# State space layer of a diffusion trunk: the tile of dt ahead of z's tiles, and out-projection weights ahead of modulation pieces in the load queue

## The chip, the cores and the metric

The kernel runs on one core of a Trainium2 chip. The metric is device time in microseconds (us), the median of several runs. Engines: PE is TensorE (matmul), DVE is VectorE, ACT is ScalarE, POOL is GpSimd, SP issues nearly all DMAs. Every engine runs its own list of instructions in order, and the lists meet only at semaphores.

## The reference, cut to what matters

Four layers, each a token mixer (pooling, state space, conformer, attention) and a convolutional feed-forward part. Two streams of tokens, 128 context and 256 latent, share the weights. The state space mixer (layer 1) and the gated residual around it:

```python
def ssd_mixer(h, h0, w_in, conv_w, conv_b, dt_bias, a_log, d_skip, norm_g, w_out):
    proj = h @ w_in                                   # 1024 -> z 2048, xbc 4096, dt 64
    z = proj[..., :SSD_D_INNER]
    xbc = jax.nn.silu(depthwise_conv(proj[..., SSD_D_INNER:SSD_D_INNER + SSD_CONV_DIM], conv_w, conv_b))
    dt = jax.nn.softplus(dt_raw + dt_bias.astype(jnp.float32))
    a = -jnp.exp(a_log.astype(jnp.float32))
    y_f, s_f = ssd_scan(x, dt[:, :, 0], a[0], bm, cm, h0[:, 0])      # and y_b, s_b backward
    y = (y_f + flip(y_b) + x * skip).reshape(bsz, seq_len, SSD_D_INNER).astype(h.dtype)
    y = rms_norm(y * jax.nn.silu(z), norm_g)
    return y @ w_out, jnp.stack([s_f, s_b], axis=1)
...
def gated_residual(x, out, mod, k, g):
    return x + mod[:, None, 3 * k + 2] * rms_norm(out, g)
```

The scan needs dt, and the cumulative sums of dt * a over each chunk of 128 tokens. It does not need z: z only multiplies the result of the scan. The conformer (layer 2) ends in a product with `conf_w_out` (1024 x 1024). The modulation `mod = silu(cond) @ w_mod[i] + b_mod[i]` is six vectors of 1024 for each layer and stream.

## The kernel before

**Products.** Every weight is fp32 and is split into a rounded high part and a low rest, and every product is three matmuls (high x high, low x high, high x low). The weights come in chunks of 128 x 1024 (512 KB; dt's is half as wide), numbered through the whole kernel by `plan()`. A ring of four slots (`raw`, `w_hi`, `w_lo`) holds them. SP loads chunk m into `raw` once both low halves of chunk m - 4 are made. ScalarE rounds it (`round_to`, L820) once chunk m - 4 has been used by TensorE. GpSimd (`low_to`, L675) and VectorE (L1179) make half of the low part each; for the conformer's weights GpSimd makes all of it. TensorE waits for both (`chunk_ready`). Each engine's calls of `round_to` and `low_to` stand at written-out places between its other work, so a wait for a chunk holds whatever stands behind it on that engine.

**State space layer.** `in_tile` makes 32 tiles for the convolution, then 16 tiles of z (24 matmuls of 386 columns each), then one of dt with 64 rows. ScalarE evacuates z with Silu into `zt` (L937), and dt with a copy (L940). `dt_prepare` is a chain through four engines: three transposes (L1767), VectorE adds the bias and forms -|v| (L1347 to L1350), ScalarE takes Exp (L945), VectorE makes the logarithm by a series (L1352 to L1363, 15 steps), TensorE makes the cumulative sums and totals (L1774, L1775), VectorE subtracts (L1369 to L1373), ScalarE takes two Exp (L947, L948), VectorE multiplies (L1375). Then 24 steps of the scan follow. Afterwards, in `ssd_end`, VectorE multiplies tile m with z (L1463) and forms its low part (L1458), ScalarE squares it (L986) and rounds it (L987), GpSimd adds up the squares (L745), and each engine makes its part of one more weight chunk per tile.

**Out-projections.** `out_product` lets a chunk of weights be the moving operand against three units of 128 tokens (two banks each). All chunks but the last four (`TAIL`) go through all units in turn, 18 matmuls of 512 columns a chunk (L1709 to L1711). The last four are done for unit 0 first, so that its residual and norm can begin (`transition`) while TensorE does units 1 and 2. In the state space layer the sum of squares over partitions (L1867) precedes chunk 12. `fill` puts the products of modulation pieces between the transposes of the transition.

**Modulation pieces.** w_mod comes in pieces of 1 MB (`load_mod`, L511), 12 for the end of one sublayer and the next. They lie in SBUF places that other buffers leave free only at certain times: slots 0 and 1 in the scan's buffers, others under `zt`, `xbc` or the conformer's tables. SP's list interleaves them with chunks of weights by hand. For the out-projection of the state space layer it is:

```python
load_to(s.n0 + 13)
sp.wait_ge(w_used, s.n0 + 6)
load_ends(2, 2, 7)
load_to(s.n0 + 15)
sp.wait_ge(y_lo_ready, KI)
load_ends(2, 4, 5, 6)
load_to(s.n0 + s.chunks)
```

For the conformer's it is four chunks, the wait `sp.wait_ge(mid_lo, KD)`, and then a chunk and two pieces in turn.

Of the kernel before, what the change touches and what calls it, by code (L numbers as in the profile page):

```python
# [11 lines left out]
ACT = mybir.ActivationFunctionType  # L12
AX = mybir.AxisListType

P = 128
D = 1024
KD = D // P
# [75 lines left out]
def plan():  # L93
    order = [Linear("pool", 2)]
    for l in range(DEPTH):
        if l == 1:
            order += [Linear("ssd_conv", CONV_TILES), Linear("ssd_z", KI), Linear("ssd_dt", 1, KD * NDT),
                      Linear("ssd_out", KI)]
        if l == 2:
            order += [Linear("conf_in", 2 * KD), Linear("conf_out", KD)]  # L100
        if l == 3:
            order += [Linear("qk", QK), Linear("v", 2), Linear("attn_out", KD)]
        order += [Linear(f"ffn_in{l}", FFN_TILES), Linear(f"ffn_out{l}", KF)]
# [34 lines left out]
def build_trunk(nc, a, out):  # L138
# [4 lines left out]
    with ExitStack() as ctx:  # L143
# [146 lines left out]
        def tile_bank(j):  # L290
            return bank((j + 2) % 4)
# [129 lines left out]
        EVAC_Z, EVAC_DT = 0, KI  # L421
# [31 lines left out]
        ALL_STEPS = list(steps())  # L453

# [48 lines left out]
        def _(sp):  # L503
# [85 lines left out]
            for n, s in enumerate(order[1:], 1):  # L589
# [23 lines left out]
                elif s.name == "ssd_out":  # L613
# [7 lines left out]
                    load_to(s.n0 + 15)  # L621
                    sp.wait_ge(y_lo_ready, KI)
                    load_ends(2, 4, 5, 6)
                    load_to(s.n0 + s.chunks)
# [42 lines left out]
        def _(pool):  # L667
# [142 lines left out]
        def _(act):  # L810
# [122 lines left out]
            def ssd_z_dt():  # L933
                s = lin["ssd_z"]
                for m in range(KI):
                    act.wait_ge(w_used, s.n0 + m + 1)
                    act.activation(zt[:, m, :], tile_bank(m)[:, 0:COLS], ACT.Silu).then_inc(evac, 1)  # L937
                    round_to(s.n0 + m + 5)
                act.wait_ge(w_used, lin["ssd_dt"].n0 + 1)
                act.activation(dt_columns, tile_bank(KI)[0:NDT, 0:COLS], ACT.Copy).then_inc(evac, 1)  # L940
# [39 lines left out]
            def ssd_end():  # L980
                n0 = lin["ssd_out"].n0
                for m in range(KI):
# [6 lines left out]
                    if m + 3 < KI:  # L989
                        round_to(n0 + m + 3)  # L990
# [139 lines left out]
            for l in range(DEPTH):  # L1130
                if l == 1:
                    ssd_conv()
                    ssd_z_dt()
                    dt_prepare()
                    scan_act()
                    round_to(lin["ssd_out"].n0 + 3)
                    ssd_end()
                    round_to(lin["ssd_out"].n0 + KI)
# [28 lines left out]
        def _(vec):  # L1167
# [154 lines left out]
            def ssd_conv():  # L1322
# [11 lines left out]
                low_to(lin["ssd_dt"].n0 + 1)  # L1334

            def dt_prepare():
# [28 lines left out]
                assert n[0] == DT_DVE - 2  # L1365
                vec.wait_ge(dt_pe, 2)
                cum = bank(7)[:, 0:192].rearrange("p (c h) -> p c h", c=3)
                total = bank(7)[:, 192:384].rearrange("p (c h) -> p c h", c=3)
# [4 lines left out]
                link(vec.tensor_tensor(to_end, full_decay, neg_cum[:, :, :], ALU.add))  # L1373
                vec.wait_ge(dt_act, 4)
# [76 lines left out]
            def ssd_end():  # L1451
# [10 lines left out]
                for m in range(KI):  # L1462
# [3 lines left out]
                    if m + 3 < KI:  # L1466
                        low_to(n0 + m + 3)
# [136 lines left out]
            for l in range(DEPTH):  # L1604
                if l == 1:
# [3 lines left out]
                    low_to(lin["ssd_out"].n0 + 3)  # L1609
                    ssd_end()  # L1610
                    low_to(lin["ssd_out"].n0 + KI)
# [20 lines left out]
        def _(ten):  # L1632
# [130 lines left out]

            def dt_prepare():
                ten.wait_ge(evac, EVAC_DT + 1)
# [3 lines left out]
                ins.then_inc(dt_pe, 1)  # L1769
                ten.wait_ge(z_dt, DT_DVE - 2)  # L1770
                cum = bank(7)[:, 0:192].rearrange("p (c h) -> p c h", c=3)
# [3 lines left out]
                ten.matmul(bank(7)[:, 192:384], ones[:, :], adt[:, :, :].rearrange("p c h -> p (c h)"),  # L1775
                           start=True, stop=True, skip_group_check=True).then_inc(dt_pe, 1)

# [63 lines left out]
            def ssd():  # L1841
                conv, z, dt = lin["ssd_conv"], lin["ssd_z"], lin["ssd_dt"]
# [5 lines left out]
                for m in range(KI):  # L1848
                    if m < 4:
                        ten.wait_ge(conv_done, conv.conv0 + CONV_TILES - 3 + m)  # L1850
                    else:
                        ten.wait_ge(evac, EVAC_Z + m - 3)
                    chunk_ready(z.n0 + m)
                    tile(tile_bank(m)[:, 0:COLS], z.n0 + m, P, slice(0, COLS)).then_inc(w_used, 1)
                chunk_ready(dt.n0)
                ten.wait_ge(evac, EVAC_Z + KI - 3)
                tile(tile_bank(KI)[0:NDT, 0:COLS], dt.n0, NDT, slice(0, COLS)).then_inc(w_used, 1)
# [337 lines left out]
```

## Time and profile before

| What | Value |
|---|---|
| Median of 3 runs | 2193.52 us (2193.38 to 2196.08) |
| Profiled execution, its own time | 2196.92 us |
| Its span, in which all rows below lie | 2195.2 us |
| PE busy | 2015.6 us, 92% |
| DVE, ACT, POOL busy | 58%, 45%, 34% |
| Read from HBM | 314.96 MB, 145 GB/s over the span |

Times in rows are microseconds from the start of the span. A busy share is an average over stages with different limits; what a change in one stage is worth is read from that stage. The state space layer's z tiles lie at 565 to 637, its scan at 651 to 798, its out-projection and transition at 798 to 917; the conformer's out-projection begins at 1364.64.

### The profile page before, as it was taken

Reading aid. Unit: us, or ns where it says so; the run is one execution under the profiler, and the core shown is the slowest. Engines: PE = TensorE matmul, PEld = TensorE weight load, DVE = VectorE, ACT = ScalarE, POOL = GpSimd, SP = SyncE. Lnnn points to the kernel's source line nnn. Section 1 sums busy time; section 2 is a strip of 40 time slices with the busy share of each in tenths; the row PEclk is TensorE's granted clock in tenths of the full one; section 3 lists DMA queues with packets and bytes.
Section 4 is the critical chain, followed back from the end, with each engine's and each line's share of the span. In section 5 each row is a group of like instructions: output and inputs, shape, how many; then the busy total and the mean of one; then the engine's idle time right before and its main releaser. Section 6 shows DMA issues by size and latency. Waiting matters only on the chain.

```text
span 2195.2 us, 30850 instructions
## 1 busy us (share of the span) xinstructions
PE 2015.6 (92%) x11973; PEld 1813.9 (83%) x11973; DVE 1279.9 (58%) x1911; ACT 994.9 (45%) x1767; POOL 747.3 (34%) x568
## 2 busy tenths in 40 slices
PE   3789999999978878899999998799999979899998
PEld 1579998799977866799987997599998766699986
DVE  0567761566328866677724795377751686577732
ACT  1344442554336633544424686354442535544432
POOL 0133324333327655333343840233334320333242
PEclk6889999999989989999999999899999988999999
DMA  9953336433310134643365500643446322243332
GB/s 370 374 212 125 125 120 244 162 121 124 125 62 26 40 120 157 237 144 122 119 225 178 196 19 1 278 173 125 125 163 220 145 109 81 86 144 125 124 126 77
DMA packets 77073, 320.98 MB, mean 146 GB/s; under 512 B 8672, under 2 KB 14208, under 8 KB 63104
## 3 DMA queue, kind: packets, MB, share of 16 engines
q1 hardware_dynamic: 76048, 318.18, 41.3%
q8 instruction: 96, 1.57, 0.3%
q10 hardware_dynamic: 880, 0.82, 0.1%
q14 instruction: 49, 0.40, 0.1%
HBM read 314.96 MB, written 4.01 MB: 145 GB/s over the span
## 4 chain that ended last, share of the span: by engine, by line
PE 77%; DVE 9%; ACT 5%; DMA 4%; issue 2%; POOL 1%; SPq 1%; DVEq 0%; ACTq 0%
PE pair L1675 16%; PE pair L1677 16%; PE pair L1676 16%; PE pair L1709 6%; PE pair L1710 6%; PE pair L1711 6%; DMA mod_more<-in_w_mod 2%; PE pair L1798 2%; DVE x L1246 2%; PE pair L1896 1%; PE pair L1895 1%; PE pair L1894 1%; PE pair L1831 1%; ACT junk L848 1%; DMA raw<-in_ssd_out 1%
## 5 line engine op out<-in xcount | busy, mean ns | idle before, releaser
L675 POOL TENSOR_TENSOR w_lo<-raw,w_hi 128x512 fp32r<-128x512 f32 (+1 forms) x375 | 578.2, 1544 | 1205.5 <-ACT w_hi L820 1205.5
L1675 PE MATMUL pair<-h_hi,w_hi 128*128 128x386 f32 (+1 forms) x2008 | 687.6, 342 | 19.1 <-POOL h_lo L682 19.1
L1677 PE MATMUL pair<-h_hi,w_lo 128*128 128x386 f32 (+1 forms) x2008 | 683.4, 340 | 0.0
L1676 PE MATMUL pair<-h_lo,w_hi 128*128 128x386 f32 (+1 forms) x2008 | 682.8, 340 | 0.0
L1179 DVE TENSOR_TENSOR w_lo<-raw,w_hi 128x512 fp32r<-128x512 f32 x351 | 426.6, 1217 | 335.9 <-ACT w_hi L820 335.9
L820 ACT ACTIVATE w_hi<-raw 128x1024 fp32r<-128x1024 f32 x375 | 393.0, 1050 | 294.2 <-PE pair L1711 213.0
L1675 PEld LDWEIGHTS pair<-h_hi,w_hi 128*128 128x128 f32 (+1 forms) x2008 | 380.6, 190 | 23.6 <-POOL h_lo L682 22.3
L1676 PEld LDWEIGHTS pair<-h_lo,w_hi 128*128 128x128 f32 (+1 forms) x2008 | 381.5, 190 | 0.9
L1677 PEld LDWEIGHTS pair<-h_hi,w_lo 128*128 128x128 f32 (+1 forms) x2008 | 380.8, 190 | 0.3
L1303 DVE SCALAR_TENSOR_TENSOR acc<-pair,taps,acc 128x385 f32<-128x385 f32 x176 | 108.9, 619 | 213.1 <-ACT acc L907 213.1
L907 ACT ACTIVATE acc<-pair,taps 128x386 f32<-128x386 f32 x176 | 117.3, 667 | 236.7 <-PE pair L1677 236.7
L1710 PE MATMUL pair<-w_hi,g 128*128 128x512 f32 x528 | 208.5, 395 | 0.0
L1711 PE MATMUL pair<-w_lo,g 128*128 128x512 f32 x528 | 208.4, 395 | 0.0
L1709 PE MATMUL pair<-w_hi,g 128*128 128x512 f32 x528 | 208.3, 395 | 0.0
L1709 PEld LDWEIGHTS pair<-w_hi,g 128*128 128x128 f32 x528 | 99.2, 188 | 23.4
L1710 PEld LDWEIGHTS pair<-w_hi,g 128*128 128x128 f32 x528 | 99.2, 188 | 23.3
L1711 PEld LDWEIGHTS pair<-w_lo,g 128*128 128x128 f32 x528 | 99.2, 188 | 23.4
L905 ACT ACTIVATE g<-gate 128x386 fp32r<-128x386 f32 x84 | 44.3, 528 | 162.4 <-DVE gate L1316 162.4
L1310 DVE SCALAR_TENSOR_TENSOR acc<-pair,taps,acc 128x385 f32<-128x385 f32 x176 | 108.5, 617 | 3.2
L1484 DVE SCALAR_TENSOR_TENSOR convolved<-glu,conf_tab,convolved 128x400 f32<-128x400 f32 x120 | 101.3, 917 | 0.0
L682 POOL TENSOR_TENSOR h_lo<-stage,h_hi 128x512 fp32r<-128x512 f32 x21 | 31.9, 1521 | 92.7 <-ACT h_hi L870 92.7
L1798 PE MATMUL pair<-mod_raw,wk 128*64 128x128 f32 x384 | 44.8, 291 | 17.9 <-DVE stage L1414 11.3
(254 smaller groups left out, 2557.1 us busy)
## 6 DMA issues: line engine op xcount, KB each, us to landing
raw<-in_ffn_in SPq DMA_DIRECT2D x176, 512.0 KB, 3.5
raw<-in_ffn_out SPq DMA_DIRECT2D x88, 512.0 KB, 3.6
mod_raw<-in_w_mod SPq DMA_DIRECT2D x32, 1024.0 KB, 7.7
mod_base<-in_w_mod SPq DMA_DIRECT2D x31, 1024.0 KB, 7.3
mod_more<-in_w_mod SPq DMA_DIRECT2D x20, 1024.0 KB, 13.8
raw<-in_ssd_conv SPq DMA_DIRECT2D x32, 512.0 KB, 3.5
gb<-rows_dram SPq DMA_DIRECT2D x8, 1024.0 KB, 5.4
raw<-in_ssd_z SPq DMA_DIRECT2D x16, 512.0 KB, 3.5
```

The source lines that it names most:

```text
L675: pool.tensor_tensor(w_lo[:, m % SLOTS, 0:w], raw[:, m % SLOTS, 0:w], w_hi[:, m % SLOTS, 0:w].bitcast(F32), ALU.subtract).then_inc(w_low_p ...
L820: act.activation(w_hi[:, m % SLOTS, 0:w], raw[:, m % SLOTS, 0:w], ACT.Copy).then_inc(w_rounded, 1)
L907: act.activation(acc[:, j % 4, :], tile_bank(j)[:, 0:COLS], ACT.Identity, scale=taps[:, l, j, 1:2], bias=taps[:, l, j, 3:4]).then_inc(acc_ ...
L1179: vec.tensor_tensor(w_lo[:, m % SLOTS, w0:w1], raw[:, m % SLOTS, w0:w1], w_hi[:, m % SLOTS, w0:w1].bitcast(F32), ALU.subtract).then_inc(w_ ...
L1303: vec.scalar_tensor_tensor(out=acc[:, j % 4, 1:COLS], in0=b[:, 0:COLS - 1], scalar=taps[:, l, j, 0:1], in1=acc[:, j % 4, 1:COLS], op0=ALU. ...
L1310: vec.scalar_tensor_tensor(out=acc[:, j % 4, 0:COLS - 1], in0=b[:, 1:COLS], scalar=taps[:, l, j, 2:3], in1=acc[:, j % 4, 0:COLS - 1], op0= ...
L1675: ten.matmul(to, wh, h_hi[:, k, cols], start=k == 0, stop=False, skip_group_check=True)
L1676: ten.matmul(to, wh, h_lo[:, k, cols], start=False, stop=False, skip_group_check=True)
L1677: ins = ten.matmul(to, wl, h_hi[:, k, cols], start=False, stop=k == KD - 1, skip_group_check=True)
L1709: ten.matmul(to, hi[:, k, cols], wh, start=first, stop=False)
L1710: ten.matmul(to, lo[:, k, cols], wh, start=False, stop=False)
L1711: ins = ten.matmul(to, hi[:, k, cols], wl, start=False, stop=last)
```

## The change

- The order of the chunks is conv, dt, z, out in place of conv, z, dt, out.
- TensorE: dt's tile goes to bank 7 right after the convolution's tiles, then z tile 0, the three transposes, z tiles 1 to 3, the cumulative sums (now in bank 5), z tiles 4 to 15. z's tiles rotate over three banks (2, 3, 7) in place of four. Before the scan TensorE waits for the last evacuation of z.
- ScalarE: dt's copy and z's Silus stand inside `dt_prepare`: Exp of a_log, copy of dt, z 0, Exp of -|v|, z 1 to 15, then the last two Exp.
- VectorE: `low_to` calls up to z chunk 5 stand after the 18 steps, and those up to the fourth out-projection chunk before the last step. ScalarE and GpSimd also handle the first four out-projection chunks before the scan (three before, of which GpSimd and VectorE made the low parts after it).
- `ssd_end`: each tile m goes with chunk `min(m + 3, KI)`, so the last chunk is made inside the loop on all three engines.
- SP, `ssd_out`: all 16 chunks are issued ahead of the wait for `y_lo_ready`; the pieces 4, 5, 6 follow it.
- SP, `conf_out`: all 8 chunks are issued ahead of the wait for `mid_lo`; the seven pieces follow it together.

```diff
-            order += [Linear("ssd_conv", CONV_TILES), Linear("ssd_z", KI), Linear("ssd_dt", 1, KD * NDT),
+            order += [Linear("ssd_conv", CONV_TILES), Linear("ssd_dt", 1, KD * NDT), Linear("ssd_z", KI),
...
-        EVAC_Z, EVAC_DT = 0, KI
+        EVAC_DT, EVAC_Z = 0, 1
...
+        def z_bank(m):
+            return bank((2, 3, 7)[m % 3])
...
-                    load_to(s.n0 + 15)
+                    load_to(s.n0 + s.chunks)
                     sp.wait_ge(y_lo_ready, KI)
                     load_ends(2, 4, 5, 6)
-                    load_to(s.n0 + s.chunks)
...
-                    load_to(s.n0 + SLOTS)
+                    load_to(s.n0 + s.chunks)
                     sp.wait_ge(mid_lo, KD)
-                    for i in range(KD - SLOTS):
-                        load_to(s.n0 + SLOTS + i + 1)
-                        load_ends(4, 2 + 2 * i, 3 + 2 * i) if i < 3 else load_ends(4, 8)
+                    load_ends(4, *range(2, MOD_SLOTS))
...
-                    if m + 3 < KI:
-                        low_to(n0 + m + 3)
+                    low_to(n0 + min(m + 3, KI))
...
-                    low_to(lin["ssd_dt"].n0 + 1)
+                    low_to(lin["ssd_out"].n0 + SLOTS)
                     pool.wait_ge(z_dt, DT_DVE)
                     scan_pool()
-                    low_to(lin["ssd_out"].n0 + 3)
                     ssd_end()
-                    low_to(lin["ssd_out"].n0 + KI)
...
+            def z_evac(m):
                 s = lin["ssd_z"]
...
+                act.wait_ge(w_used, s.n0 + m + 1)
+                act.activation(zt[:, m, :], z_bank(m)[:, 0:COLS], ACT.Silu).then_inc(evac, 1)
+                round_to(s.n0 + m + 5)
 
             def dt_prepare():
                 act.activation(rowc[:, 960:1024], dt_rows[:, 1, :], ACT.Exp).then_inc(dt_act, 1)
+                act.wait_ge(w_used, lin["ssd_dt"].n0 + 1)
+                act.activation(dt_columns, bank(7)[0:NDT, 0:COLS], ACT.Copy).then_inc(evac, 1)
+                round_to(lin["ssd_dt"].n0 + 5)
+                z_evac(0)
                 act.wait_ge(z_dt, 3)
                 act.activation(rowc[:, 576:768], rowc[:, 384:576], ACT.Exp, scale=-1.0).then_inc(dt_act, 1)
+                for m in range(1, KI):
+                    z_evac(m)
                 act.wait_ge(z_dt, DT_DVE - 1)
...
-                low_to(lin["ssd_dt"].n0 + 1)
+                low_to(lin["ssd_z"].n0 + 4)
...
+                low_to(lin["ssd_z"].n0 + 6)
                 vec.wait_ge(dt_pe, 2)
...
                 link(vec.tensor_tensor(to_end, full_decay, neg_cum[:, :, :], ALU.add))
+                low_to(lin["ssd_out"].n0 + SLOTS)
                 vec.wait_ge(dt_act, 4)
...
+            def z_tiles(first, last):
+                z = lin["ssd_z"]
+                for m in range(first, last):
+                    if m < 2:
+                        ten.wait_ge(conv_done, lin["ssd_conv"].conv0 + CONV_TILES - 3 + m)
+                    else:
+                        ten.wait_ge(evac, EVAC_Z + m - 2 if m > 2 else EVAC_DT + 1)
+                    chunk_ready(z.n0 + m)
+                    tile(z_bank(m)[:, 0:COLS], z.n0 + m, P, slice(0, COLS)).then_inc(w_used, 1)
+
             def dt_prepare():
+                dt = lin["ssd_dt"]
+                chunk_ready(dt.n0)
+                tile(bank(7)[0:NDT, 0:COLS], dt.n0, NDT, slice(0, COLS)).then_inc(w_used, 1)
+                z_tiles(0, 1)
                 ten.wait_ge(evac, EVAC_DT + 1)
...
                 ins.then_inc(dt_pe, 1)
+                z_tiles(1, 4)
                 ten.wait_ge(z_dt, DT_DVE - 2)
...
                            start=True, stop=True, skip_group_check=True).then_inc(dt_pe, 1)
+                z_tiles(4, KI)
+                ten.wait_ge(evac, EVAC_Z + KI)
```

## Rows read from the trace of the kernel before

**Rows 1.** The page's chain that ended last, by engine

```profile
PE 77%; DVE 9%; ACT 5%; DMA 4%; issue 2%; POOL 1%; SPq 1%; DVEq 0%; ACTq 0%
```

**Rows 2.** Windows: length, busy PE, PEld, DVE, ACT, POOL (count), PEclk, DMA share, GB/s

```profile
564.87:637.15 72.28, 72.25 (x408) 70.94 (x407) 11.53 (x16) 25.17 (x36) 23.87 (x14) 1.00 0.35 113
637.15:650.69 13.54, 2.25 (x9) 1.64 (x10) 8.66 (x24) 3.00 (x6) 0.00 (x0) 0.68 0.00 0
868.17:884.48 16.31, 10.85 (x31) 8.57 (x32) 0.87 (x2) 1.32 (x3) 1.76 (x1) 0.71 1.00 404
869.45:873.86 4.41, 4.41 (x12) 3.44 (x12) 0.18 (x1) 0.26 (x1) 0.00 (x0) 0.50 1.02 427
1371.14:1383.60 12.46, 12.46 (x54) 9.97 (x53) 1.05 (x4) 2.48 (x4) 2.75 (x2) 1.00 0.83 329
1385.00:1400.97 15.97, 7.71 (x20) 5.26 (x20) 0.00 (x1) 2.11 (x2) 5.31 (x3) 0.64 1.01 420
```

**Rows 3.** Timeline of all engines, last z tile to scan: start, us, instruction, idle before

```profile
637.15 0.49 ACT L940 ACTIVATE stage<-pair 64x386 f32<-64x386 f32 x1 [2.77 <-PE pair L1677]
637.66 1.28 ACT L943 ACT_TABLE_LOAD   x1
...
638.13 0.36 DVE L1347 TENSOR_TENSOR rowc<-pair,dt_rows 128x192 f32<-128x192 f32 x1 [16.48 <-PE pair L1767]
...
639.67 0.26 DVE L1352 TENSOR_SCALAR rowc<-rowc 128x192 f32<-128x192 f32 x1 [0.50 <-ACT rowc L945]
...
645.87 0.36 DVE L1363 SCALAR_TENSOR_TENSOR adt<-rowc,dtv 128x192 f32<-128x192 f32 x1
...
646.29 1.17 PE L1774 MATMUL pair<-adt,tri 128*128 128x96 f32 x4 [8.20 <-DVE adt L1363]
...
648.25 0.36 DVE L1369 TENSOR_SCALAR neg_cum<-pair 128x192 f32<-128x192 f32 x1 [2.02 <-PE pair L1775]
...
649.47 0.36 ACT L947 ACTIVATE stage<-stage 128x192 f32<-128x192 f32 x1 [9.90 <-DVE stage L1373]
...
650.69 0.45 PE L1819 MATMUL pair<-ident,xbc 128*128 128x128 f32 x1 [2.55 <-DVE stage L1375]
```

**Rows 4.** Timeline of ScalarE, one of 16 z tiles

```profile
573.39 0.49 ACT L937 ACTIVATE zt<-pair 128x386 f32<-128x386 f32 x1 [2.81 <-PE pair L1677]
573.78 1.05 ACT L820 ACTIVATE w_hi<-raw 128x1024 fp32r<-128x1024 f32 x1
```

**Rows 5.** Timeline, out-projection of the state space layer

```profile
844.34 1.04 ACT L820 ACTIVATE w_hi<-raw 128x1024 fp32r<-128x1024 f32 x1
...
846.02 1.66 DVE L1463 TENSOR_TENSOR xbc<-xbc,zt 128x386 f32<-128x386 f32 x1
...
862.52 0.60 ACT L987 ACTIVATE y_hi<-xbc,ssd_cols 128x386 fp32r<-128x386 f32 x1
...
863.27 1.22 DVE L1463 TENSOR_TENSOR xbc<-xbc,zt 128x386 f32<-128x386 f32 x1
...
884.48 1.11 ACT L837 ACTIVATE junk<-pair,ssd_inv 128x1024 bf16<-128x1024 f32 x1 [4.92 <-PE pair L1711]
...
891.55 1.04 ACT L820 ACTIVATE w_hi<-raw 128x1024 fp32r<-128x1024 f32 x1
```

**Rows 6.** Chain that ended last, in order of time, both out-projections: start, us, what

```profile
800.26 10.27 DMA raw<-in_ssd_out
...
868.70 9.78 DMA raw<-in_ssd_out
...
1376.58 17.87 DMA raw<-in_conf_out
...
1400.97 1.24 DVE wk L1233
```

**Rows 7.** Timeline of SP and of GpSimd, conformer's out-projection

```profile
1252.58 119.96 SPq L520 DMA_DIRECT2D raw<-in_conf_out  x5
...
1395.61 2.34 POOL L675 TENSOR_TENSOR w_lo<-raw,w_hi 128x1024 fp32r<-128x1024 f32 x1 [3.83 <-ACT w_hi L820]
```

More of the change, by code:

```diff
@@ L931, in ssd_conv @@
                 act.activation(xbc[:, CONV_TILES - 1, :], xbc[:, CONV_TILES - 1, :], ACT.Silu).then_inc(xbc_ready, 1)
-            def ssd_z_dt():
+            def z_evac(m):
                 s = lin["ssd_z"]
[L935 to L940, printed above, removed]
+                act.wait_ge(w_used, s.n0 + m + 1)
+                act.activation(zt[:, m, :], z_bank(m)[:, 0:COLS], ACT.Silu).then_inc(evac, 1)
+                round_to(s.n0 + m + 5)
             def dt_prepare():
                 act.activation(rowc[:, 960:1024], dt_rows[:, 1, :], ACT.Exp).then_inc(dt_act, 1)
+                act.wait_ge(w_used, lin["ssd_dt"].n0 + 1)
+                act.activation(dt_columns, bank(7)[0:NDT, 0:COLS], ACT.Copy).then_inc(evac, 1)
+                round_to(lin["ssd_dt"].n0 + 5)
+                z_evac(0)
                 act.wait_ge(z_dt, 3)
                 act.activation(rowc[:, 576:768], rowc[:, 384:576], ACT.Exp, scale=-1.0).then_inc(dt_act, 1)
+                for m in range(1, KI):
+                    z_evac(m)
                 act.wait_ge(z_dt, DT_DVE - 1)
@@ L988, in ssd_end @@
                                    ).then_inc(y_hi_ready, 1)
-                    if m + 3 < KI:
-                        round_to(n0 + m + 3)
+                    round_to(n0 + min(m + 3, KI))
                 act.wait_ge(y_sum, 1)
@@ L1132, in _ @@
                     ssd_conv()
-                    ssd_z_dt()
                     dt_prepare()
                     scan_act()
-                    round_to(lin["ssd_out"].n0 + 3)
                     ssd_end()
-                    round_to(lin["ssd_out"].n0 + KI)
                     transition(2, lin["ffn_in1"].n0)
@@ L1365, in dt_prepare @@
                 assert n[0] == DT_DVE - 2
+                low_to(lin["ssd_z"].n0 + 6)
                 vec.wait_ge(dt_pe, 2)
-                cum = bank(7)[:, 0:192].rearrange("p (c h) -> p c h", c=3)
-                total = bank(7)[:, 192:384].rearrange("p (c h) -> p c h", c=3)
+                cum = bank(5)[:, 0:192].rearrange("p (c h) -> p c h", c=3)
+                total = bank(5)[:, 192:384].rearrange("p (c h) -> p c h", c=3)
                 ch.did(vec.tensor_scalar(neg_cum[:, :, :], cum, -1.0, None, ALU.mult))
@@ L1465, in ssd_end @@
                         y_low(m - 1)
-                    if m + 3 < KI:
-                        low_to(n0 + m + 3)
+                    low_to(n0 + min(m + 3, KI))
                 y_low(KI - 1)
@@ L1608, in _ @@
                     scan_dve()
-                    low_to(lin["ssd_out"].n0 + 3)
                     ssd_end()
-                    low_to(lin["ssd_out"].n0 + KI)
                     transition(2, lin["ffn_in1"].n0)
@@ L1769, in dt_prepare @@
                 ins.then_inc(dt_pe, 1)
+                z_tiles(1, 4)
                 ten.wait_ge(z_dt, DT_DVE - 2)
-                cum = bank(7)[:, 0:192].rearrange("p (c h) -> p c h", c=3)
+                cum = bank(5)[:, 0:192].rearrange("p (c h) -> p c h", c=3)
                 for d in range(2):
@@ L1774, in dt_prepare @@
                     ten.matmul(cum[:, :, hs], tri[:, d, :], adt[:, :, hs], start=True, stop=True, skip_group_check=True)
-                ten.matmul(bank(7)[:, 192:384], ones[:, :], adt[:, :, :].rearrange("p c h -> p (c h)"),
+                ten.matmul(bank(5)[:, 192:384], ones[:, :], adt[:, :, :].rearrange("p c h -> p (c h)"),
                            start=True, stop=True, skip_group_check=True).then_inc(dt_pe, 1)
+                z_tiles(4, KI)
+                ten.wait_ge(evac, EVAC_Z + KI)
             def scan_pe():
@@ L1841, in ssd @@
             def ssd():
-                conv, z, dt = lin["ssd_conv"], lin["ssd_z"], lin["ssd_dt"]
+                conv = lin["ssd_conv"]
                 in_start(1)
@@ L1847, in ssd @@
                     in_tile(conv, j, 1)
[L1848 to L1857, printed above, removed]
                 dt_prepare()
```

## The prediction

> **What bounds the kernel now.** I read the chain of work that ended last first [rows 1]: TensorE carries most of it, so a gain has to come from places where TensorE stands still. The busy time by windows [rows 2] shows three such places that the diff touches. Between the last column tile of the state space layer and its scan, 13.54 us hold 2.25 us of matmuls. In its out-projection 16.31 us hold 10.85 us with the DMA engines full. In the conformer's out-projection 15.97 us hold 7.71 us, again with the DMA full. A row of the timeline or the chain then names what ended each wait. All three are serial chains: softplus on ScalarE and VectorE [rows 3], and twice a weight that sits in the queue behind modulation pieces [rows 6].
>
> **Softplus (dt first).** Today TensorE's last product matmul is evacuated at 637.15 and the scan starts at 650.69 [rows 3]: 13.5 us.
>
> What moves: dt's tile costs TensorE the same wherever it stands (17 tiles fill 72.28 us, 4.25 each [rows 2]). Its evacuation, the transposes, 18 VectorE steps and one Exp go under z's tiles. What must hold is that they are done by the time TensorE has z tile 3 behind it. With TensorE's conv tiles ending at 564.87: dt ends at 569.1, z tile 0 at 573.4, the transposes at about 574. Three VectorE steps and the Exp took from 638.13 to 639.67, 1.5 us [rows 3]; up to two table loads of 1.28 come on top. The chain from L1352 to L1363 runs from 639.67 to about 646.25, so 6.6 us [rows 3]. It ends near 583 to 585; z tiles 1 to 3 end at 574.2 + 3 x 4.25 = 586.9. Slack 2 to 4 us, so no stall.
>
> Queued behind it: VectorE's low halves of z chunks 4 and 5, done near 586; they are wanted at 588 and 592. SP's loads of z chunks 8 and 9 wait for them; chunk 8 is first rounded after tile 4 (about 592). ScalarE's rounding waits for the three VectorE steps once, and is otherwise four chunks ahead; a z tile costs it 1.44 us of 4.25 [rows 4], so three banks in place of four and two more table loads fit. I cost these at nothing; were the cover gone, each late us would be paid once.
>
> What stays visible. (a) Between z tiles TensorE now does the transposes and the cumulative sums. The sums took 646.29 to 648.25, 1.96 us, at half clock (the window's granted clock is 0.68 of full [rows 2, 3]). At full clock half of that, 1.0, plus 0.5 for the transposes: 1.5 us, bounds 1.0 and 2.5. (b) After z tile 15: its Silu 0.5, the rounding of an out-projection chunk 0.95 [rows 4], a table load 1.28 since Exp follows Silu, and then the steps that today run from 649.47 to 650.69, 1.22 us [rows 3]. Sum 4.0 us, with 3.7 and 6 as bounds (the VectorE low half of that chunk stands in the same queue before the last product).
> Gain 13.5 - 1.5 - 4.0 = **8.0 us** (5.0 to 8.8).
> The change loads tables five times here, where today it is once (Exp, Silu, Exp, Silu, Exp), and one load stands in the open; the row gives a load 1.28 us, from 637.66 to 638.94 [rows 3]. The Trainium skill (ScalarE: Activation LUTs, Rules for kernel authors) speaks against that: do all functions of one table set before switching, and budget about 2.7 us for a switch. By that figure, an estimate from that page, the open tail would be 1.4 us longer and the whole gain 22.9.
>
> **Out-projection of the state space layer.** VectorE's three low halves at its start leave the end of the scan for z's time. It gains nothing: the next weight, chunk 4, comes behind the gate row and two modulation pieces, 10.27 us after its issue at 800.26 [rows 6]. VectorE's queue blocks on it (its low half stands before the product of tile 3), and SP's order there is untouched. So TensorE merely waits longer, and chunks 2 to 11 keep their times.
>
> The last chunk is another matter. Its load is issued after y_lo's last tile and three pieces, lands 9.78 us later at 878.48, and lets the first output unit start its square at 884.48 [rows 5, 6]. Now it is issued when low half 11 is done (about 847, within 3 us of the rounding at 844.34), so it is there when its slot comes free. The price: its rounding and low halves move in front of y's tiles 14 and 15. ScalarE is free for it at 862.52 + 0.5 = 863.05, when chunk 11 has just been used. From a rounding over the low half to the next VectorE product it takes 846.02 - 844.34 = 1.68 us, so tile 14's product moves from 863.27 to 864.73 [rows 5]. With GpSimd on the same buffers, the two products take about 1 us more: 2.4 us, bounds 1.5 and 3.5. The sums' matmul, with which the window at 868.17 begins, goes to 870.6; 1.3 us later the 24 matmuls of unit 0 begin, the first ten at half clock: the ten that start in the window took 4.41 us (it counts two of the sums' too), and warm 54 took 12.46, so 0.233 each with the edges [rows 2]. 870.6 + 1.3 + 4.4 + 14 x 0.233 + 0.2 for the last one's end = 879.8. Gain 884.48 - 879.8 = **4.7 us** (3 to 6).
> Next late: the first ffn_in weight, behind five pieces whose issue moves with y_lo, 2 to 3 us later than today. 5.8 MB at the 404 GB/s of that window [rows 2] plus some 2 us from 870.5 is 887; ScalarE wants it 891.55 - 884.48 = 7.1 us after unit 0's square [rows 5], near 887. Even, at most 1 us lost.
>
> **Out-projection of the conformer.** Chunks 4 to 7 are each issued in turn with two pieces between them; the last is issued at 1376.58 and lands 17.87 us later [rows 6]. SP issued the first chunks from 1252 on, and the fifth only after the wait on mid_lo, 120 us later [rows 7]. Without that order the slots are free from the low half of chunk 3 on, some 90 us before they are wanted. What paces it then is TensorE itself: the first phase ends at 1383.6 [rows 2]. Chunk 7 is rounded from 1383.8, 1.05; its low half takes GpSimd 2.34 [rows 7]; ready at 1387.3. Unit 0's chunks 4 to 6 are 18 x 0.233 = 4.2 and reach 1387.8, so no wait; six more end at 1389.4. VectorE starts on unit 0 at 1389.4 in place of 1400.97 [rows 6]. From there VectorE and ScalarE pace the transition, so the whole of it moves: **11.6 us** (bounds 9, if half the low halves come late, and 12).
> Next late: the seven pieces, 7.3 MB at 420 GB/s [rows 2], from 1374.3 to 1391.8; today they end later. The first is used after units 1 and 2, 48 matmuls or 11 us after 1389.4 at the soonest, so they cost nothing. The first ffn_in chunk follows by 1393; by the other transition's 7.1 us it is wanted at 1396.5 or later.
>
> **Sum.** 8.0 + 4.7 + 11.6 = 24.3 us. The profiled execution took 2196.92 us for a span of 2195.2, so about 2172.6 after. It lies 3.4 above the median of the runs, against which the forecast stands: 2193.52 - 24.3 = **2169.2 us**, -1.1%.
>
> **Rivals.**
> 1. All three gains, as above: 0.60. Its own range 2166 to 2173.
> 2. The softplus chain surfaces (ScalarE's waits and four table loads hold z's roundings, or the tail has another step): the layer's first gain falls to 3. For it: the slack is only 2 to 4 us, and the chain's two-input steps share time with GpSimd's low halves. Against: one delay is paid once, not per tile. 2193.52 - 19.3 = 2174. Chance 0.15.
> 3. Earlier weights, but the pieces become the wait: both transitions use their pieces soon after. In the conformer the margin is 10 us and in the state space layer about 0 for the first ffn_in weight. Were half of the 16.3 us there given back: 2177.5. Chance 0.10.
> 4. More than forecast: TensorE stands still for only 4 us before the scan, and 8 us of half clock at several restarts go away. The ten slow matmuls of a restart cost 10 x 0.2 = 2 us each, two or three places: 2164. Chance 0.10.
> 5. Slower: VectorE's low halves of z chunks 4 and 5 now stand behind the softplus chain, and TensorE, then every later z tile, waits for them. It decides once the chain ends more than 24 us past 586.9, near 611; the chain would have to take 33 us where 6.6 are measured. At 10 us beyond that point the time is 2203. Chance 0.03.
> 6. None shows, because other stages take it back (a wait that ends at the same time for another reason): 2193. For it speaks that two of the three gains lie in one layer; against, that the chain there names one releaser at a time. Chance 0.02.
>
> **How the numbers follow.** Cases 1 to 4 reach from 2164 to 2177.5 and hold 0.95; leaving out the outer ends of 3 and 4 about 0.85 remains in 2164.5 to 2177. Faster by over 0.2%: 0.95. Within 0.2% (4.4 us, about what a measurement of this kernel can tell from no change): 0.02. Slower: 0.03.
>
> **What would show it.** Scan's first transposes near 642.5 to 644 in place of 650.69, with a table load on ScalarE just before; z tiles without gaps but for one of 1 to 2 us after tile 3; the last ssd_out load issued near 840 to 848 less the shift, and no TensorE wait on a GpSimd low half of 5 us before unit 0; four conf_out loads before 1300 and no wait for them after the first phase. It would be wrong if a z tile waited on a low half, if the tail after z tile 15 exceeded 6 us, or if the first ffn_in weight landed late.

## The result and the profile after

The changed kernel takes 2167.8 us, median of four runs from 2167.5 to 2168.1, beside 2193.5 (2190.3 to 2196.1) for the kernel before in the same measurement: ratio 0.9884, 95% interval 0.9867 to 0.9901, or 25.6 us. The forecast was 2169.2, 24.3 us. Measured again it was 2166.6 beside 2194.3: 0.9873 (0.9858 to 0.9888).

The chain that ended last, by engine, in the page of the changed kernel; it answers to [rows 1]:

```profile
PE 80%; DVE 6%; ACT 4%; issue 3%; DMA 3%; POOL 3%; SPq 1%; DVEq 0%; ACTq 0%; POOLq 0%
```

TensorE's share rose from 77 to 80%. VectorE's fell from 9 to 6%, the DMA's from 4 to 3, and GpSimd's rose from 1 to 3. The windows of the changed kernel (columns as in [rows 2]) show where:

```profile
562.77:636.33 73.56, 73.52 (x417) 71.99 (x415) 25.00 (x41) 31.34 (x42) 28.19 (x17) 1.00 0.36 115
636.33:640.23 3.90, 0.00 (x0) 0.03 (x1) 1.16 (x3) 3.33 (x5) 1.77 (x1) 0.95 0.00 0
858.37:868.02 9.65, 9.65 (x32) 7.94 (x33) 0.45 (x2) 0.98 (x2) 0.00 (x0) 0.65 0.85 336
1369.43:1373.86 4.43, 4.43 (x20) 3.58 (x20) 0.00 (x0) 0.00 (x0) 2.41 (x1) 1.00 0.99 418
```

z's stretch has VectorE 13.5 us busier than before and TensorE without a gap (73.52 of 73.56). The 13.54 us before the scan are 3.90, the 16.31 before unit 0's square 9.65 with TensorE busy throughout, and the conformer's second phase, in which unit 0 gets its last four chunks, runs to VectorE's first instruction at full clock in 4.43 us.

The tail, changed kernel, timeline of all engines; it answers to [rows 3]:

```profile
636.33 0.49 ACT L933 ACTIVATE zt<-pair 128x386 f32<-128x386 f32 x1 [2.81 <-PE pair L1672]
636.72 1.05 ACT L817 ACTIVATE w_hi<-raw 128x1024 fp32r<-128x1024 f32 x1
637.78 1.28 ACT L947 ACT_TABLE_LOAD   x1
...
639.08 0.36 ACT L947 ACTIVATE stage<-stage 128x192 f32<-128x192 f32 x1
639.35 0.35 ACT L948 ACTIVATE stage<-stage 128x192 f32<-128x192 f32 x1
639.73 0.36 DVE L1373 TENSOR_TENSOR stage<-stage,dtv 128x192 f32<-128x192 f32 x1 [1.24 <-ACT stage L948]
...
640.23 0.45 PE L1831 MATMUL pair<-ident,xbc 128*128 128x128 f32 x1 [3.94 <-DVE stage L1373]
```

Each start lies within 0.15 us of the end of the row above: the tail is a plain sum, 3.9 us, where 4.0 were forecast. VectorE's low half of the same chunk (637.80, 0.69 us) lies beside the table load and adds nothing.

The two out-projections, changed kernel, timelines of SP's queue, ScalarE, VectorE and TensorE; they answer to [rows 5, 6, 7]:

```profile
825.97 9.67 SPq L523 DMA_DIRECT2D raw<-in_ssd_out  x3
858.37 1.41 PE L1869 MATMUL pair<-ones,stage 128*128 128x1 f32 x6 [7.60 <-POOL stage L744]
868.02 1.11 ACT L834 ACTIVATE junk<-pair,ssd_inv 128x1024 bf16<-128x1024 f32 x1 [7.95 <-PE pair L1706]
...
1237.39 31.65 SPq L523 DMA_DIRECT2D raw<-in_conf_out  x8
1357.06 3.60 SPq L514 DMA_DIRECT2D mod_base<-in_w_mod  x7
1368.36 1.06 ACT L817 ACTIVATE w_hi<-raw 128x1024 fp32r<-128x1024 f32 x1 [3.26 <-PE pair L1706]
1373.86 1.23 DVE L1229 TENSOR_TENSOR wk<-pair,rowc 128x1024 f32<-128x1024 f32 x1 [16.83 <-PE pair L1706]
```

The last ssd_out weight leaves with its neighbours at 826 to 836, not after the last tile. The eight conf_out weights leave between 1237 and 1269, ahead of the pieces at 1357; the last rounding waits for TensorE, no longer for a DMA.

### The profile page after: what moved, and what is told of

Same layout as the page of the kernel before. It is cut to its first block, busy times and chain, and to the rows that moved or that the text cites. A ratio compares the mean times of both kernels' runs of the same rounds, so it can differ in the third digit from the quotient of the medians.

```text
span 2166.2 us, 30854 instructions
## 1 busy us (share of the span) xinstructions
PE 2010.2 (93%) x11973; PEld 1810.5 (84%) x11973; DVE 1279.4 (59%) x1911; ACT 999.7 (46%) x1771; POOL 747.4 (35%) x568
## 4 chain that ended last, share of the span: by engine, by line
PE 80%; DVE 6%; ACT 4%; issue 3%; DMA 3%; POOL 3%; SPq 1%; DVEq 0%; ACTq 0%; POOLq 0%
PE pair L1670 17%; PE pair L1672 16%; PE pair L1671 16%; PE pair L1704 6%; PE pair L1705 6%; PE pair L1706 6%; PE pair L1810 2%; DVE x L1242 1%; DMA mod_more<-in_w_mod 1%; PE pair L1897 1%; PE pair L1898 1%; PE pair L1896 1%; POOL w_lo L675 1%; PE pair L1843 1%; DMA raw<-in_pool 1%
```

## Experiments

Medians of kernels from different measurements differ by a few us for one and the same code, so stretches of one profiled execution say more. Each column is a difference between the starts of two instructions. A: first evacuation behind the conv tiles to the scan's first transpose. B: from there to VectorE's last output of the scan. C: to the square of unit 0. D: the conformer's out-projection, first matmul to VectorE's first instruction of unit 0. E: first evacuation to the last residual. "In place of" and "shorter" always mean such distances, not the absolute times.

```
                                    median us   A      B       C      D      E
kernel before                       2193.5    81.55  147.16  86.63  36.33  1621.70
changed kernel                      2167.8    73.24  145.84  81.95  24.39  1594.83
r1_change_again                     2166.6    73.24  145.50  82.98  24.47  1595.66
e1_conformer_loads                  2183.6    81.55  147.57  84.15  24.76  1612.34
e2_last_chunk                       2188.5    81.54  147.38  79.58  36.23  1615.34
e3_dt_first                         2186.5    73.24  145.60  86.96  36.18  1614.54
e4_loads_before_scan                2163.2    73.24  145.73  76.24  25.17  1591.22
e5_tail_reordered                   2166.4    72.30  145.49  79.82  24.39  1591.33
e6_sums_two_tiles_early             2175.9    81.08  144.99  81.90  24.45  1601.70
e7_tables_under_cover               2169.0    73.24  145.49  82.99  24.42  1595.64
e8_two_tables_in_the_open           2172.1    76.25  145.97  83.01  24.48  1599.17
e9_early_loads_short_tail           2162.8    72.29  145.56  77.67  24.38  1588.12
e10_warm_matmuls                    2186.6    74.95  145.72  79.96  25.55  1618.36
e11_with_warm_matmuls               2165.1    74.95  144.26  78.09  24.51  1591.37
```

The first four experiments ran together (before: 2194.0). Three are one part of the change each.

**e1_conformer_loads**

```diff
-                    load_to(s.n0 + SLOTS)
+                    load_to(s.n0 + s.chunks)
                     sp.wait_ge(mid_lo, KD)
-                    for i in range(KD - SLOTS):
...
+                    load_ends(4, *range(2, MOD_SLOTS))
```

> The kernel before with one part of the change alone: in the conformer's out-projection all eight weight chunks are issued before the wait on mid_lo, the seven pieces together behind it. Theory (the whole of the late weights comes back, and the transition behind moves with it): unit 0 starts on VectorE 11.6 to 12 us earlier, and the time is 11.6 to 12 us less than the kernel before, near 2181.7 us. Rival (the pieces become the wait): half of it or less, 4 to 6 us, 2188 us, with VectorE or GpSimd waiting for a modulation piece in that transition.

Ratio 0.9955 (0.9941 to 0.9968), 10.5 us between the medians. D fell by 11.57. The interval, 7 to 13 us, holds the theory's 11.6 to 12 and leaves out the rival's 4 to 6. In the transition behind, no instruction of VectorE, ScalarE or TensorE waited for a DMA: the theory holds.

**e2_last_chunk**

```diff
-                    load_to(s.n0 + 15)
+                    load_to(s.n0 + s.chunks)
                     sp.wait_ge(y_lo_ready, KI)
                     load_ends(2, 4, 5, 6)
-                    load_to(s.n0 + s.chunks)
```

and on ScalarE, VectorE and GpSimd the loop's `if m + 3 < KI:` gives way to `min(m + 3, KI)`.

> The kernel before with one part alone: the last chunk of the state space layer's out-projection is issued with the others, and its rounding and low halves come in the loop over y's tiles. Theory: unit 0's square comes 4.7 us earlier, counted from the end of the scan, at a price of 2.2 us on the sums' matmul; about 1.3 us of it is given back in the next linear's first tile, which starts cold. Time 3.4 to 4.7 us less than before, 2189 to 2190 us. Rival A (the 1.3 us belong to the profile's own spread): the whole 4.7, and the first ffn_in1 tile's matmuls at the spacing they have before. Rival B (the first ffn_in weight lands late behind the pieces): less than 2 us.

Ratio 0.9974 (0.9964 to 0.9984), 5.6 us. From the sums' matmul (the sum of squares over partitions, ahead of chunk 12) to the square it takes 9.49 us in place of 16.31; the price is TensorE's wait for the sums, 7.60 in place of 5.38. That is 4.6 net, and C is 4.57 shorter than in e1, whose code is that of before there. (Beside the kernel before C is 7.05 shorter, but TensorE's clock differs there: behind its wait before chunk 2 it ran at half clock in the kernel before, at full clock in e1 and e2.) The theory's other half fell: the next linear's first tile to the next residual takes 271.43 us, as before (271.42). In e1, where nothing differs, it takes 272.93. So the 1.3 to 1.5 us that seemed to be given back are a spread of one and the same code. In 3 of the 14 profiled executions (before, e2, e9) TensorE started this tile at full clock and the stretch took 271.4 us; in the other 11 it started at half clock and took 272.7 to 273.0.

**e3_dt_first**: the whole diff but for SP's two orders and the last chunk.

> The kernel before with dt's tile first and softplus under z's tiles, as in the change, but with the load order of both out-projections as before. Theory: the scan's first transposes come 8.3 us earlier and the scan itself is 1.3 us shorter, since its first step no longer starts cold: 9.6 us in all, 2183.8 us, and with the other two parts about 25, so the parts add up. Rival (softplus alone gives 8.0 to 8.3 and the scan's 1.3 us came from elsewhere): 8.2 us, 2185.2, and 16 matmuls of the scan's first step take 3.4 us as before.

Ratio 0.9963 (0.9951 to 0.9976), 7.5 us. The median is nearer to the rival's, but the interval, 5 to 11 us, holds both, so the stretches must decide. A fell by 8.31, to the hundredth as in the changed kernel. B is 1.6 to 2.0 shorter than in the three kernels without this part. A and B together give 9.9, the theory's 9.6. They do not reach the end: C is 0.3 longer than before (2.8 longer than in e1, where TensorE kept its full clock), from unit 0's square to ffn_in's first tile it takes 29.37 us in place of 28.29, and that tile is one of those at half clock, which costs 1.5.

B's gain comes at the scan's two ends. The scan's first step takes 3.64 us to the second one's first transpose, before 4.51. The sixteen matmuls that the rival names take 2.71 in place of 3.62, against it, but the first transposes are 0.21 us apart as before (0.11 at full clock, in e10): TensorE still starts at half clock. The larger part comes from the scan's end. Before, timeline of GpSimd, VectorE and TensorE:

```profile
786.43 2.78 DVE L1443 TENSOR_TENSOR mod_raw<-mod_raw,stage 128x512 f32<-128x512 f32 x2 [0.77 <-ACT mod_raw L978]
786.96 4.78 POOL L675 TENSOR_TENSOR w_lo<-raw,w_hi 128x512 fp32r<-128x512 f32 x3
...
789.65 0.97 DVE L1409 TENSOR_TENSOR stage<-state,stage 128x256 f32<-128x256 f32 x1
...
791.33 1.09 PE L1798 MATMUL pair<-mod_raw,wk 128*64 128x128 f32 x4 [5.65 <-DVE stage L1414]
```

and the changed kernel:

```profile
776.81 1.71 DVE L1441 TENSOR_TENSOR mod_raw<-mod_raw,stage 128x512 f32<-128x512 f32 x2 [0.77 <-ACT mod_raw L978]
...
778.96 0.41 DVE L1407 TENSOR_TENSOR stage<-state,stage 128x256 f32<-128x256 f32 x1
...
780.08 1.09 PE L1810 MATMUL pair<-mod_raw,wk 128*64 128x128 f32 x4 [4.03 <-DVE stage L1412]
```

GpSimd's three low halves ran beside VectorE's last products of the scan. With the halves moved to z's time these rows are 1.07 and 0.56 us shorter, and TensorE's wait falls by 1.62. No run moves these halves alone, so the cause is argued from the rows; but the short durations stand in all eleven profiled executions with dt first, the long ones in all three without. In e3 the two ends give 3.1 us, and 1.5 of it is lost again in the steps between (127.3 us from the second step to the last, before 125.8), for a reason that stays open; r1 has no such loss (125.7).

**e4_loads_before_scan**

```diff
-                    load_to(s.n0 + SLOTS)
+                    load_to(s.n0 + 2 * SLOTS)
                     scan_traffic()
```

> The changed kernel, with chunks 4 to 7 of the state space layer's out-projection issued before the scan, in place of behind the gate row and two pieces. Theory (that load, 10 us behind its issue, is what makes the low halves moved to z's time worth nothing): with it gone VectorE no longer blocks on chunk 4's rounding, TensorE does not stand 4 us before chunk 2, and the time is 3 to 5 us less than that of the changed kernel, 2163 to 2165 us. Rival (VectorE's own work for each y tile paces the first tiles, and the load is hidden): chunk 2 starts at most 1 us earlier, and the time is that of the changed kernel, 2167.8 us.

TensorE's longer waits in the first tiles, first the changed kernel and then this one:

```profile
789.19 0.47 PE L1704 MATMUL pair<-w_hi,y_hi 128*128 128x512 f32 x1 [3.17 <-DVE y_lo L1456]
803.30 0.47 PE L1704 MATMUL pair<-w_hi,y_hi 128*128 128x512 f32 x1 [4.05 <-DVE y_lo L1456]
```

```profile
788.77 0.47 PE L1704 MATMUL pair<-w_hi,y_hi 128*128 128x512 f32 x1 [3.17 <-DVE y_lo L1456]
799.59 0.47 PE L1704 MATMUL pair<-w_hi,y_hi 128*128 128x512 f32 x1 [0.78 <-DVE y_lo L1456]
```

The wait of 4.05 is 0.78, C is 5.7 us shorter than in the changed kernel (6.7 than in r1), and the time is 2163.2: 0.9861 (0.9848 to 0.9875) of before. Chunk 2 starts 3.3 us nearer to the scan's end, and TensorE then runs at full clock in place of half. So chunk 4's load is what kept the moved low halves from bringing anything here. The run moves the loads of chunks 5 to 7 as well, so it does not show chunk 4's alone.

The next four ran together (before: 2194.3).

> The changed kernel once more, on the same chip as the next three, so that they can be compared with it. Its parts measured alone gave 10.5, 5.6 and 7.5 us, 23.6 together, and the first measurement of the whole 25.6: 2168 to 2170 us is expected.

**e5_tail_reordered**

```diff
-                for m in range(1, KI):
+                for m in range(1, KI - 1):
                     z_evac(m)
+                act.wait_ge(w_used, lin["ssd_z"].n0 + KI)
+                act.activation(zt[:, KI - 1, :], z_bank(KI - 1)[:, 0:COLS], ACT.Silu).then_inc(evac, 1)
                 act.wait_ge(z_dt, DT_DVE - 1)
                 act.activation(to_end, to_end, ACT.Exp).then_inc(dt_act, 1)
                 act.activation(full_decay, full_decay, ACT.Exp).then_inc(dt_act, 1)
+                round_to(lin["ssd_out"].n0 + SLOTS)
```

and the low halves of that chunk in the loop.

> The changed kernel with ScalarE's rounding of the out-projection's fourth chunk behind the two last Exps in place of ahead of them (and that chunk's low halves in the loop over y's tiles). Theory (every term of the tail stands in series): the 1.05 us of the rounding leave it, the scan's first transpose starts 2.9 us behind z tile 15's Silu in place of 3.9, and the time falls by 1 us. Rival (the low halves of that chunk, put back into the loop, cost the out-projection as much): the scan starts 1 us earlier and the time stays.

The tail lost 0.94 us, as a plain sum must. The time, 2166.4 beside 2166.6, does not resolve it, and E is 4.3 less than in r1 while C alone is 3.2 less: chunk 4 was rounded 11.93 us after the scan's last output in place of 12.60, and behind its wait of 2.83 us before chunk 2 TensorE ran at full clock, where r1 had waited 5.70 and ran at half. C spreads over 3.1 us in the six executions whose code is that of the changed kernel there (79.96 in e10 to 83.01 in e8), so whether the reordering is worth more than its 0.94 us stays open.

**e8_two_tables_in_the_open**: a one-column Exp and a one-column Silu ahead of the last two Exps.

> The changed kernel with a one-column Exp and a one-column Silu ahead of the last two Exps, where nothing covers them: two more table loads in the tail. Theory (a load costs its own 1.28 us of the row and nothing else): the tail is 2.6 us longer, plus 0.3 to 0.5 for the two small activations, so 2.9 to 3.1 us in all. Rival: each switch costs more than its load, so that the tail grows by 4 us or more and an idle stretch shows before or behind each load. By a separate sentence on the Trainium skill (ScalarE: Activation LUTs, Rules for kernel authors), whose figure is about 2.7 us a switch, the growth would be an estimated 5.4 us.

ScalarE's timeline:

```profile
636.33 1.28 ACT L947 ACT_TABLE_LOAD   x1
...
637.63 0.21 ACT L947 ACTIVATE junk<-eps_col 128x1 bf16<-128x1 f32 x1
637.84 1.28 ACT L948 ACT_TABLE_LOAD   x1
639.13 0.20 ACT L948 ACTIVATE junk<-eps_col 128x1 bf16<-128x1 f32 x1
639.34 1.28 ACT L949 ACT_TABLE_LOAD   x1
640.64 0.36 ACT L949 ACTIVATE stage<-stage 128x192 f32<-128x192 f32 x1
```

A grew by 3.01 us: two loads of 1.28 and the two activations, nothing between them. The median grew by 5.5 beside r1, more than the stretches show (E: 3.5). The two profiled executions, 2170.81 and 2165.76, are 5.05 apart, and 1.6 of that lies ahead of the first evacuation, where the code is the same. The medians by themselves could not tell 3.0 from the estimate of 5.4; the rows do.

**e6_sums_two_tiles_early**: `z_tiles(1, 2)` before the sums, `z_tiles(2, KI)` after.

> The changed kernel with the cumulative sums behind z tile 1 in place of z tile 3, so that TensorE must wait for the softplus chain: the sums come about 575.7 us, the chain ends at 582.1. Theory (one delay is paid once, as the prediction held against its second rival): TensorE stands 6 to 6.5 us once, starts again at half clock for up to 2 us more, and no later z tile waits; the time grows by 6 to 8.5 us. Rival (the delay also holds back VectorE's low halves of z chunks 4 and 5 and from them every later tile): waits at z tiles 4 to 8 as well, and over 10 us.

```profile
582.42 1.17 PE L1784 MATMUL pair<-adt,tri 128*128 128x96 f32 x4 [6.12 <-DVE adt L1359]
```

It is TensorE's only wait over 0.1 us from 560 us to the tail. A grew by 7.84: the wait and 1.7 us of half clock behind it (granted clock 0.77 from 582 to 590). The median is 9.3 us over r1's, above the expected 6 to 8.5; E is 6.0 over it, and 3.35 of the distance between the two profiled executions (9.35) lies ahead of the first evacuation again. One delay is paid once, and no later tile waits.

The last four ran together too (before: 2194.3).

**e7_tables_under_cover**: a one-column Exp behind each of z tiles 4 to 11.

> The changed kernel with a one-column Exp behind each of z tiles 4 to 11 on ScalarE: sixteen more table loads (20.5 us by the row of 1.28) and eight small activations under z's tiles. Theory (a z tile costs ScalarE 1.44 us of 4.25, and the loads are covered): the scan's first transpose keeps its distance of 73.2 us from dt's evacuation, no z tile waits, and the time stays within 1 us. Rival (ScalarE's roundings come late): waits of TensorE at z tiles, some us in all.

A is 73.24 and E 1595.64, as in r1: sixteen loads under z's tiles cost nothing. The median is 1.2 us over the changed kernel's first one and 2.4 over r1's, from other measurements; the ratio to before is 0.9884 (0.9868 to 0.9900), that of the first measurement.

**e10_warm_matmuls**

```diff
                 z_tiles(4, KI)
+                for i in range(26):
+                    ten.matmul(bank(4)[:, 0:P], ones[:, :], tri[:, 0, :], start=True, stop=True, skip_group_check=True)
```

> The changed kernel with 26 matmuls of 128x128 whose result nobody reads, put behind z tile 15 where TensorE waits 3.9 us for the tail. Theory (the scan's first step is slow because TensorE's clock falls while it stands): the five transposes and products start spaced 0.11 in place of 0.22 us and the sixteen matmuls behind them take 1.95 in place of 2.9 us, so the scan's second step comes about 1.5 us earlier. Rival (the first step waits on its inputs, whatever the clock): no difference.

TensorE's timeline:

```profile
634.11 5.97 PE L1789 MATMUL pair<-tri,ones 128*128 128x128 f32 x52
...
640.46 1.95 PE L1845 MATMUL pair<-tri,adt 128*128 128x128 f32 x16
```

The sixteen matmuls did fall to 1.95 us from 2.87 (3.51 in r1), and the second step's first transpose came 2.34 us after the first step's, in place of 3.80 and 3.99: the clock is what slows the first step, worth 1.5 us. But each f32 matmul appears as two, 52 in 5.97 us where the tail has 3.9, and the scan started 1.7 us late, which takes it back. Half as many should fit, by an estimate from the 5.97; this was not run. The time came out in two groups: 3 of 12 runs from 2163.8 to 2169.7, 9 from 2185.8 to 2192.1. The profiled one is of the second. From ffn_in's first tile to the conformer's out-projection it takes 474.9 us, r1 453.3. The code there is that of the changed kernel, and 19.0 of the 21.6 us are one wait of TensorE in the conformer's input linear. GpSimd and VectorE there:

```profile
1226.38 27.03 POOL L675 TENSOR_TENSOR w_lo<-raw,w_hi 128x1024 fp32r<-128x1024 f32 x1 [3.99 <-ACT w_hi L817]
...
1225.47 25.74 DVE L1481 SCALAR_TENSOR_TENSOR convolved<-glu,conf_tab,convolved 128x400 f32<-128x400 f32 x47
```

and in r1:

```profile
1225.32 2.66 POOL L675 TENSOR_TENSOR w_lo<-raw,w_hi 128x1024 fp32r<-128x1024 f32 x1 [2.77 <-ACT w_hi L817]
...
1225.64 46.47 DVE L1481 SCALAR_TENSOR_TENSOR convolved<-glu,conf_tab,convolved 128x400 f32<-128x400 f32 x33
```

The first low half stood 27 us, while 45 of the 47 VectorE instructions started, 0.55 us apart; in r1 the two take turns, and a VectorE instruction comes every 1.4 us. TensorE waited 18.99 us for that weight (to 1253.51).

**e9_early_loads_short_tail**: e4 and e5 together, with `load_to(s.n0 + 2 * SLOTS - 1)`.

> The two edits together: the rounding of the out-projection's fourth chunk behind the last Exps, and chunks 4 to 6 of it issued before the scan. Theory: the gains add up, 4 to 5 us of the early loads and 0.9 of the tail, so 2161 to 2163 us. Rival (the fourth chunk's low halves back in the loop cost what the tail gives): 2163 to 2164.

2162.8 us, 0.9854 (0.9841 to 0.9867) of before, and E 1588.12, the least of all, though half of the 3.1 us by which it is below e4's is ffn_in's first tile at full clock (271.4 us for that stretch, in e4 272.95). The medians do not separate it from e4 (2163.2), so the rival is not excluded; both are faster than the change by 3.4 to 5 us.

**e11_with_warm_matmuls**: e9 with the 26 matmuls of e10.

> The same two edits and the 26 unread matmuls as well. Theory: 1 to 1.5 us less than without them, near 2160.5 us, if the clock stays up over the tail. Rival: no difference, or some tenths more, if the matmuls delay the scan's first transpose.

The same two groups: 5 of 9 runs from 2159.3 to 2165.1, 4 from 2185.5 to 2187.4. The profile shows no gain over e9 (E 3.3 more), but it is of the slowest of the five. Their median is 2162.3, e9's 2162.8. So a gain of 1 to 1.5 us is neither shown nor excluded, and the second group makes the kernel slower as a whole (median 2165.1).

## Why the prediction was right, step by step

- **Softplus, 8.0 us**: 8.31. Visible between z tiles were 0.33 for the transposes and 0.77 for the sums, 1.1 where 1.5 were forecast. The tail was 3.9 for 4.0. The slack, forecast as 2 to 4, was 2.2 us: the chain ended at 582.1 and the sums started at 584.32. e6 confirms the price of missing it, against rivals 2 and 5. Timelines of VectorE and TensorE, changed kernel:

```profile
571.13 0.40 PE L1776 MATMUL pair<-ident,stage 64*128 64x64 f32 x3
571.46 0.44 PE L1670 MATMUL pair<-h_hi,w_hi 128*128 128x386 f32 x1
...
581.72 0.36 DVE L1359 SCALAR_TENSOR_TENSOR adt<-rowc,dtv 128x192 f32<-128x192 f32 x1
...
584.32 0.58 PE L1784 MATMUL pair<-adt,tri 128*128 128x96 f32 x4
```

- **Table loads**: the row's 1.28 us decided. The Trainium skill (ScalarE: Activation LUTs, Rules for kernel authors) gives about 2.7 us a switch; two switches in the open took 3.01 with their activations (e8), not 5.4, and sixteen under cover nothing (e7).
- **Moved low halves, "It gains nothing"**: right for the stretch that the step speaks of, and incomplete. The step overlooked GpSimd's half of them, which by the rows cost VectorE's last products of the scan 1.6 us. B fell by 1.2 to 2.2 us in the kernels with dt first (2.9 in e11), about as much as the whole forecast was short of the first measurement. Behind the scan chunk 4's load did what the prediction said of it: counted from the scan's end, chunk 2 started after 17.2 us, before after 17.5 (in e1 16.6), and TensorE merely waited longer, 4.05 us in place of 2.69 (5.70 in r1).
- **Last chunk, 4.7 us**: 4.57 between e2 and e1, whose clocks agree. Between the profile before and after the square comes 6.66 us nearer to the sums' matmul, at a price of 2.2 (forecast 2.4), so 4.4; r1 gives 4.2. C as a whole fell by 4.68, and by 3.65 in r1, other waits included.
- **First ffn_in weight**, at most 1 us lost: ScalarE waited 0.68 us for it; the stretch from unit 0's square to that linear did not grow (28.29 to 28.24).

```profile
875.78 1.06 ACT L817 ACTIVATE w_hi<-raw 128x1024 fp32r<-128x1024 f32 x1 [0.68 <-DMA raw<-in_ffn_in]
```

- **Conformer, 11.6 us**: 11.94 (11.86 in r1), and 11.57 alone (e1). The pieces left at 1357.06, forecast for 1374.3, less the 15.2 by which all was earlier there, 1359.1; nothing waited for them; rival 3 did not occur.
- **Sum, 24.3 us**: 25.6 and 27.7 in two measurements; the parts alone give 10.5 + 5.6 + 7.5 = 23.6, each with some 2 to 3 us of uncertainty. In the two profiles E fell by 26.9 and 26.0: on average A 8.3, B 1.5, C 4.2, D 11.9, which is 25.9. The spans, 2195.2 and 2166.2, differ by 29.0; 2.1 of it lies at the start, which varies by 5 us between executions (first evacuation at 563.97 to 569.14). That the sum came within 1.3 us in the first measurement is in part luck: B's 1.5 us were not in it, C gave up to 1 us less than forecast, and ffn_in's first tile, at half clock in both profiles of the changed kernel and at full in the one before, lost 1.3 to 1.4.
- **Rival 4, restarts at half clock that go away (2164)**: they did not. TensorE still starts the scan at half clock or falls to it within the first step, and runs at half clock behind the wait before chunk 2. e10 shows what a restart costs in the scan's first step, 1.5 us.

## What to carry to other kernels

Moving an engine's side work off the end of a stage can help the engine that runs beside it even where its own queue gains nothing; look at the neighbour's durations, not only at waits. A weight that must be there when a stage begins belongs in the queue before the long stage ahead of it, not behind the traffic that the stage's end releases (3.4 to 4.6 us here, e4). A serial chain hidden under another's matmuls is worth what no longer stands in the open, here 8.3 of 13.5 us, as long as its slack is measured; missing the slack is paid once. A stretch of identical code should be compared between executions before a change is charged with it.

## What the runs showed of the hardware

- GpSimd's subtract of 128x1024 stood 27.03 us while 45 consecutive VectorE instructions with two SBUF inputs started (e10), where it takes 2.66 in r1; it ended 2.2 us after the last of them. The raw weight landed 1.1 us later than in the execution that went well. The Trainium skill (SBUF — State Buffer, SBUF: two separate sides) calls the pair of ports that the two engines share an exclusive lock for one instruction at a time; the trace agrees that one blocks the other, and shows besides that the blocked one need not be next. Only one of the 13 runs that were 20 us slower has a profile, so that this is the cause of the others is likely and not shown. All 13 are of the two kernels with the unread matmuls (13 of 21 runs); the eight other kernels with dt first had none in 37 runs, the change measured twice included. How the matmuls, some 590 us earlier, bring it about was not settled.
- Behind a wait of TensorE the clock came out at either of its levels, full (2.4 GHz) or half (1.2), and the wait's length alone did not say which. It had been at full before each of these. Before chunk 2 the waits and the clock behind them were:

```profile
815.31 0.47 PE L1709 MATMUL pair<-w_hi,y_hi 128*128 128x512 f32 x1 [2.69 <-DVE y_lo L1458]
810.43 0.47 PE L1707 MATMUL pair<-w_hi,y_hi 128*128 128x512 f32 x1 [1.70 <-DVE y_lo L1456]
801.50 0.47 PE L1707 MATMUL pair<-w_hi,y_hi 128*128 128x512 f32 x1 [2.83 <-DVE y_lo L1459]
```

  These are the kernel before, e1 and e5. The granted clock over the next 5 us was 0.66, 1.00 and 1.00. With the waits of 3.9 to 5.7 us in other kernels it was 0.51 to 0.66, with those of 0.7 to 1.6 and of 2.31 (e10) 1.00. The stretch from chunk 2 to the sums took 52.86 us in the kernel before and 51.31 in e1, whose code is the same there. At the start of ffn_in, behind a wait of 2.5 to 2.8 us, 17.2 us held 98 matmuls at 1.00 in the kernel before (e2 and e9 alike) and 89 at 0.90 in e1 (the others within 0.02).
- A table load is issued ahead of its activation's wait. In the changed kernel the one for z tile 0's Silu ran from 568.44 while that tile was still being multiplied, and the Silu started at 571.24:

```profile
568.44 1.28 ACT L933 ACT_TABLE_LOAD   x1
571.24 0.49 ACT L933 ACTIVATE zt<-pair 128x386 f32<-128x386 f32 x1 [1.51 <-PE pair L1672]
```
